# Centred value tiles, regrouped layer-norm steps and rotary partners moved by DMA in a two-block transformer kernel

## The reference

```python
def rotary(x, pos):                 # block 1: all 64 dims of a head, half = 32
    ...
    x1, x2 = x[..., :half], x[..., half:]
    out = jnp.concatenate([x1 * cos - x2 * sin, x2 * cos + x1 * sin], axis=-1)

def retention(q, k, v, g):          # 6 heads of 64
    q, k = rotary(q), rotary(k) * HEAD_DIM ** -0.5
    ...
    y = (y_intra + y_cross).reshape(b, s, RET_HEADS, HEAD_DIM)   # both linear in v
    y = layer_norm(y).reshape(b, s, RET_WIDTH)      # mean and variance over the 64 dims of a head
    return (jax.nn.silu(g) * y)

def hybrid_layer(x, ...):           # block 1
    u = rms_norm(x, g_mix_pre) @ w_in
    aq, ak, av, cu, rq, rk, rv, rg = jnp.split(u, SPLITS, axis=-1)
    mix = jnp.concatenate([chunk_attention(aq, ak, av, rel_bias),
                           conv_module(cu, ...),      # layer_norm over 256, then silu
                           retention(rq, rk, rv, rg)], axis=-1) @ w_out
    x = x + rms_norm(mix, g_mix_post)
    f = jnp.square(jax.nn.relu(rms_norm(x, g_mlp_pre) @ w_up)) @ w_down
    return x + rms_norm(f, g_mlp_post)

def rope(x, pos, rot_dim):          # block 2, NSA: rot_dim = 16 of a head's 64, half = 8
    xr = x[..., :rot_dim]; x1, x2 = xr[..., :half], xr[..., half:]
    rot = jnp.concatenate([x1 * cos - x2 * sin, x2 * cos + x1 * sin], axis=-1)
    return jnp.concatenate([rot, x[..., rot_dim:]], axis=-1)

def second_block(x, ...):           # each of its two layers
    x = x + 0.5 * swiglu(rmsnorm(x, ffn1_norm[l]), ...)
    ...   # mixer: MLA (6 heads), NSA (6 query heads, 2 key heads: compressed, selected, window), stick-breaking (4 heads)
    x = x + 0.5 * swiglu(rmsnorm(x, ffn2_norm[l]), ...)
```

## Time and profile before

| | before |
|---|---|
| median of three runs | 3349.65 us (3349.09 to 3351.13) |
| profiled execution, its own time | 3350.39 us |
| span of the profiled execution | 3348.6 us |
| mixing of block 1, layer 0, to the start of the output product | about 24 to 236 us |
| first layer of block 2: first MLP from, mixing | about 1283 us, 1660 to 1950 us |
| distance from layer 0 to layer 1, block 1 and block 2 | 626 us and 1033 us |

### The profile page before, as it was taken

The page is one execution under the profiler, slowest core; times in us unless marked ns, Lnnn a source line. Parts: engine busy times, 40 slices in busy tenths (PEclk is TensorE's granted clock), DMA queues, the critical chain, the costliest instruction groups (busy, mean ns, idle before and its releaser), DMA issues.

```text
span 3348.6 us, 41894 instructions
## 1 busy us (share of the span) xinstructions
PE 3295.5 (98%) x15570; PEld 2590.8 (77%) x15570; DVE 1673.7 (50%) x2170; ACT 1229.7 (37%) x1842; POOL 245.8 (7%) x268
## 2 busy tenths in 40 slices
PE   9999999999999999999999999999999999999999
PEld 6767888776678887888876788888888876678887
DVE  6755443577544335443656554435443464654434
ACT  4343122433522234223455442334332355543323
POOL 1200000021010000000102300002000101300000
PEclk9999999999999999999999999999999999999999
DMA  7213323321233232332331133333333331033332
GB/s 175 69 48 91 95 95 99 94 82 51 69 103 100 94 106 73 98 97 97 88 75 29 36 103 96 98 94 98 98 94 101 94 82 39 25 90 97 96 96 73
DMA packets 434261, 288.21 MB, mean 86 GB/s; under 512 B 44528, under 2 KB 412316, under 8 KB 433896
## 3 DMA queue, kind: packets, MB, share of 16 engines
q1 hardware_dynamic: 431272, 280.06, 28.8%
q0 software_dynamic: 2736, 4.58, 0.9%
q10 hardware_dynamic: 144, 2.10, 0.2%
HBM read 284.56 MB, written 2.13 MB: 86 GB/s over the span
## 4 chain that ended last, share of the span: by engine, by line
PE 93%; DVE 3%; ACT 2%; issue 1%; DMA 0%; SPq 0%; DVEq 0%; ACTq 0%
PE bank L2077 27%; PE bank L2079 27%; PE bank L2078 27%; PE bank L2240 2%; PE bank L2289 1%; PE bank L2264 1%; PE bank L2370 1%; PE bank L2333 1%; PE bank L2189 1%; ACT wsplit L970 1%; PE bank L2213 0%; PE bank L2101 0%; PE bank L2148 0%; PE bank L2664 0%; PE bank L2396 0%
## 5 line engine op out<-in xcount | busy, mean ns | idle before, releaser
L2077 PE MATMUL bank<-hh,wsplit 128*128 128x512 f32 x2768 | 1093.9, 395 | 10.9 <-DVE wsplit L1451 4.6
L2079 PE MATMUL bank<-hh,wsplit 128*128 128x512 f32 x2768 | 1079.0, 390 | 0.0
L2078 PE MATMUL bank<-hl,wsplit 128*128 128x512 f32 x2768 | 1078.4, 390 | 0.0
L1451 DVE TENSOR_TENSOR wsplit<-raw,wsplit 128x1024 fp32r<-128x1024 f32 (+2 forms) x534 | 645.4, 1210 | 292.9 <-ACT wsplit L970 278.3
L970 ACT ACTIVATE wsplit<-raw 128x1024 fp32r<-128x1024 f32 (+2 forms) x534 | 546.3, 1034 | 262.0 <-PE bank L2079 261.5
L2077 PEld LDWEIGHTS bank<-hh,wsplit 128*128 128x128 f32 x2768 | 520.4, 188 | 136.0 <-issue 22.9
L2078 PEld LDWEIGHTS bank<-hl,wsplit 128*128 128x128 f32 x2768 | 520.6, 188 | 109.9 <-issue 3.1
L2079 PEld LDWEIGHTS bank<-hh,wsplit 128*128 128x128 f32 x2768 | 520.2, 188 | 109.7
L2077 PE MATMUL bank<-fshi,wsplit 128*128 128x512 f32 x1294 | 507.0, 392 | 2.2 <-DVE wsplit L1451 1.4
L2079 PE MATMUL bank<-fshi,wsplit 128*128 128x512 f32 x1294 | 503.6, 389 | 0.0
L2078 PE MATMUL bank<-fslo,wsplit 128*128 128x512 f32 x1294 | 503.5, 389 | 0.0
(11 more groups left out here) (273 smaller groups left out, 2551.5 us busy)
## 6 DMA issues: line engine op xcount, KB each, us to landing
raw<-in_ffn_w_gate SPq DMA_DIRECT2D x88, 512.0 KB, 3.8
raw<-in_ffn_w_up SPq DMA_DIRECT2D x88, 512.0 KB, 3.8
raw<-in_ffn_w_down SPq DMA_DIRECT2D x88, 512.0 KB, 3.5
raw<-in_w_in SPq DMA_DIRECT2D x78, 512.0 KB, 4.0
raw<-in_w_up SPq DMA_DIRECT2D x64, 512.0 KB, 4.0
raw<-in_w_down SPq DMA_DIRECT2D x64, 512.0 KB, 3.3
raw<-in_w_out SPq DMA_DIRECT2D x16, 512.0 KB, 3.7
raw<-in_w_in SPq DMA_DIRECT2D x18, 256.0 KB, 3.3
```

What stands on the lines that cost most here:

```text
L1451: dve.tensor_tensor(slot3(wlo, s, m), slot3(raw, s, m), slot3(whi, s, m).bitcast(F32), ALU.subtract).then_inc(c.lo_done.sem, 1)
L2077: pe.matmul(o, wh, ah, start=start, stop=False)
L2078: pe.matmul(o, wh, al, start=False, stop=False)
L2079: return pe.matmul(o, wl, ah, start=False, stop=stop)
```

## The change

Three things are changed, and both order strings with them.

1. **Joints.** At the start of block 1's MLP and of block 2's first MLP, `hi` of the two units after the first stretch stands ahead of the norm on ACT, and their `lo` ahead of the first evacuations on DVE (`split=4` in block 2; block 2's second MLP stays as it is).
2. **End of block 1's mixing.** The retention's value tile is turned by products with `centre`, the identity minus `blk`, instead of transposes, so that the values and their sums have mean zero in each head. The groups `lm` go. ACT squares bank 7 in `r_out` before it copies it. The steps behind are put in another order: the three norms' groups come earlier, the two units of `ahead` are split, the silu table is loaded once ahead of the convolution's silu, the gate's silu follows, `early` 1 and 2 stand behind it, and the Ln table is loaded once at the end. A piece of attention values moves ahead.
3. **Front of block 2.** For nq0, nq1, nq2 and nks the group `swap` goes. Pool waits for ACT's copy and issues four DMAs of 8 rows each (2 KB a row) from the tile into a scratch tile of two; DVE's `roll` waits for them and does the same three operations. PE waits for `rolled` before the compressed scores (three) and before the first scores (four). nkc and nkw stay as products.

```diff
+ROLLED, ROLL_AT, ROTARY_ROWS = ("q0", "q1", "q2", "ks"), (0, 512), 8
...
-    "bffsfkfkrsekbkfkeyesrftbfcrskktfbfvyrksktefbfvskkkkfercbtyrefvkbkstkffvoseftcvrbhfkkeyhstfvrbhhhehkrhsfktcfhvbehkhstfykv"
...
+    "bffsffkkrkesbkfkeebsrftyfrcsbktfkfvyrkstekfbfvkeskfkkrkctbryvfkteskbffvorbfctvheksekyfhstfrbvherhhhkstchfkfhvbehhsktfhhv"
...
+    c[:, C_CENTRE:C_CENTRE + P] = np.eye(P) - c[:, C_BLK:C_BLK + P]
...
+                add_turned(f"rv{t}", 2432 + 128 * t, t, 4, dst=A_RV, centred=True), ("g", f"sk{t}")]
...
-    prepared += [("mix", 0), gate(0), ("mix", 1), ("g", "lm0"), ("g", "cm"), gate(1), ("mix", 2), ("g", "lv0"), ("c_square",), gate(2), ("g", "cv"), ("g", "lm1"), ("early", 0), ("g", "lv1")]
-    prepared += [("ahead",), ("early", 1), ("g", "lm2"), ("gated",), ("r_square", 2), ("rmul", 0), ("rmul", 1), ("early", 2)]
-    prepared += [("conv_out",), ("mix", 3), ("mix", 4), ("ln_set",), ("g", "lv2"), ("mix", 5), ("mix", 6), ("rmul", 2), ("mix", 7)]
+    prepared += [("mix", 0), gate(0), ("mix", 1), ("g", "cm"), gate(1), ("mix", 2), ("g", "lv0"), ("c_square",), gate(2), ("ahead", 2), ("g", "cv"), ("g", "lv1"),
+                 ("early", 0), ("ahead", 3), ("g", "lv2"), ("silu_set",), ("conv_out",), ("mix", 3), ("mix", 4), ("gated",), ("rmul", 0), ("rmul", 1), ("early", 1), ("early", 2), ("mix", 5), ("mix", 6), ("rmul", 2), ("mix", 7), ("ln_set",)]
...
-    fill += [("g", "snkc"), ("px", 0), nsa_q(0), ("px", 1), compress(0, 0), nsa_q(1), ("g", "snq0"), compress(0, 1), ("px", 2), nsa_q(2),
-             ("g", "snq1"), ("g", "cs0"), compress(1, 0), ("px", 3)]
-    fill += [add("nks", "fm", ("w_in", 1056), frees="act", dst=N_KS), ("g", "snq2"), ("g", "w20"), compress(1, 1)]
-    fill += [add("gatesf", "fm", ("w_gates_pe", 0), frees="act", dst=M_POSX), ("g", "cs1"), ("g", "snks"), ("g", "w21")]
+    fill += [("g", "snkc"), ("px", 0), nsa_q(0), ("px", 1), compress(0, 0), nsa_q(1), ("roll", 0), compress(0, 1), ("px", 2), nsa_q(2),
+             ("roll", 1), ("g", "cs0"), compress(1, 0), ("px", 3)]
+    fill += [add("nks", "fm", ("w_in", 1056), frees="act", dst=N_KS), ("roll", 2), ("g", "w20"), compress(1, 1)]
+    fill += [add("gatesf", "fm", ("w_gates_pe", 0), frees="act", dst=M_POSX), ("g", "cs1"), ("roll", 3), ("g", "w21")]
...
+                pool.wait_ge(c.rn_rstd.sem, c.rn_rstd.at(l, 2))
+                for i, name in enumerate(ROLLED):
+                    made = b2["groups"][f"n{name}"]
+                    pool.wait_ge(c.evac(made).sem, c.emptied(l, made))
+                    if i >= 2:
+                        pool.wait_ge(c.rolled.sem, c.rolled.at(l, i - 1))
+                    for head in (0, HD):
+                        for to, at in ((head, head + ROTARY_ROWS), (head + ROTARY_ROWS, head)):
+                            pool.dma_start(g(ROLL_AT[i % 2], S, (to, to + ROTARY_ROWS)), g(rolled_tile(i), S, (at, at + ROTARY_ROWS))).then_inc(c.roll_in[i % 2].sem, 16)
...
+                        act.activation(g(A_RK + S * s[1]), bank[:, 7, :], ACT.Square).then_inc(c.ret_sq.sem, 1)
                         act.activation(g(A_RQ + S * s[1]), bank[:, 7, :], ACT.Copy).then_inc(c.r_o.sem, 1)
...
-                rms_of_parts(c, l, 3, A1_MLP[1], c.mlp_parts, c.mlp_total, OUT_BANK)
                 for j in range(LOOK, 4):
                     hi(c, b, l, n0 + j + LOOK)
+                rms_of_parts(c, l, 3, A1_MLP[1], c.mlp_parts, c.mlp_total, OUT_BANK)
...
+                for n in range(LOOK, 4):
+                    hi(c, b, l, n + LOOK)
                 if l:
                     rms(c, l, 1, A_FIRST, KT, bank[:, DOWN_BANK, :], D)
                 else:
                     rms_of_parts(c, l, 1, A_FIRST[1], c.in_parts, c.in_total, DOWN_BANK)
-                mlp(l, 0, 0)
+                mlp(l, 0, 0, 4)
...
+            def roll(c, l, i):
+
+                tile, rolled = g(rolled_tile(i)), g(ROLL_AT[i % 2])
+                dve.wait_ge(c.roll_in[i % 2].sem, c.roll_in[i % 2].at(l, 4 * (i // 2) + 4))
+                dve.tensor_tensor(rolled, rolled, tab[:, S:2 * S], ALU.mult).then_inc(c.dve_step.next(), 1)
+                dve.tensor_tensor(tile, tile, tab[:, 0:S], ALU.mult).then_inc(c.dve_step.next(), 1)
+                dve.wait_ge(c.dve_step.sem, c.dve_step.now(l))
+                dve.tensor_tensor(tile, rolled, tile, ALU.add).then_inc(c.rolled.sem, 1)
...
+                    if first:
+                        for j in range(LOOK, 4):
+                            lo(c, b, l, n0 + j + LOOK, i)
                     for j in range(4):
-                        if not (first and j < LOOK):
+                        if not first:
                             lo(c, b, l, n0 + j + LOOK, i)
...
+                pe.wait_ge(c.rolled.sem, c.rolled.at(l, NSA_PAIRS))
...
+                        if gr.get("centred"):
+                            ins = pe.matmul(bk[:, P * t:P * t + P], g(gr["tile"] + P * t, P), centre, start=True, stop=True)
+                        else:
+                            ins = pe.transpose(bk[:, P * t:P * t + P], g(gr["tile"] + P * t, P), ident)
...
-                elif kind == "rmean":
-                    tile = g(A_RQ + S * gr["t"])
-                    dve.tensor_tensor(tile, tile, bk[:, :], ALU.subtract).then_inc(evac, 1)
...
-                elif kind == "rmean":
-                    pe.wait_ge(c.r_o.sem, c.r_o.at(l, 1 + gr["t"]))
-                    ins = pe.matmul(bk[:, :], blk, g(A_RQ + S * gr["t"]), start=True, stop=True)
...
+                    pe.wait_ge(c.ret_sq.sem, c.ret_sq.at(l, gr["t"] + 1))
+                    pe.wait_ge(c.r_o.sem, c.r_o.at(l, gr["t"] + 1))
                     ins = pe.matmul(bk[:, :], blk, g(A_RK + S * gr["t"]), start=True, stop=True)
```

More of the change, by code:

```diff
@@ L57 @@
 C_STACK = C_VALID + 4
-C_WORDS = C_STACK + HD
+C_CENTRE = C_STACK + HD
+C_WORDS = C_CENTRE + P
 SCR_SQ, SCR_RSTD, SCR_TMP, SCR_SQ2 = 0, 1024, 1536, 2560
@@ L657, in counts_of @@
             c.px = signal("px", 0, 4)
+            c.roll_in = [signal(f"roll_in{s}", 0, 2 * len(ROLLED), 0, 16) for s in range(2)]
+            c.rolled = signal("rolled", 0, len(ROLLED))
             c.px_hi = signal("px_hi", 0, 4)
@@ L1313, in _, with mlp @@
             c, b = c2, b2
-            def mlp(l, n0, f0):
+            def mlp(l, n0, f0, split=LOOK):
                 def gated(i, first=False):
@@ L1319, in gated @@
                     for j in range(4):
-                        if not (first and j < LOOK):
+                        if not (first and j < split):
                             hi(c, b, l, n0 + j + LOOK, i)
@@ L1885, in _ @@
                     elif s[0] == "ahead":
-                        for n in range(LOOK, OUT_FIRST + 1):
-                            lo(c, b, l, b["wo"] + n)
+                        lo(c, b, l, b["wo"] + s[1])
                 for m in range(KT):
@@ L1931, in _, with mlp @@
             c, b = c2, b2
-            def mlp(l, n0, f0, d0, r):
+            def mlp(l, n0, f0, d0, r, split=LOOK):
                 def gated(i, first=False, last=False):
                     for j in range(4):
-                        if not (first and j < LOOK):
+                        if not (first and j < split):
                             lo(c, b, l, n0 + j + LOOK, i)
@@ L1971, in _ @@
                 c.dve_step.k = 0
-                mlp(l, 0, 0, 0, 1)
+                for n in range(LOOK, 4):
+                    lo(c, b, l, n + LOOK)
+                mlp(l, 0, 0, 0, 1, 4)
                 dve.wait_ge(c.prm_in.sem, c.prm_in.at(l, 11))
@@ L1992, in _ @@
                         key_pe(c, b, l)
+                    elif s[0] == "roll":
+                        roll(c, l, s[1])
                     elif s[0] == "turn_q":
```

45 lines of the change are left out of this document (21 added, 24 removed).

## The result

| | before | after |
|---|---|---|
| median | 3350.18 us (3349.09 to 3351.13, 4 runs) | 3327.41 us (3326.95 to 3328.22, 4 runs) |
| span of the profiled execution | 3348.6 us | 3325.1 us |

The ratio is 0.9932, with a 95% interval of 0.9915 to 0.995: 22.8 us faster, where 19.1 had been forecast (3330.6, range 3322 to 3343).

A forecast was written before the change was run, and what follows sets the result against it. PE was taken to bound the kernel, busy for 3295.5 of 3348.6 us. The terms 4.1 - 3.3 + 11.8 + 0.7 + 5.8 sum to 19.1 us won, giving 3330.6, range 3322 to 3343.

The forecast's parts named there:

- joints: MLP entries: PE's waits for low parts go, 2.6 us in block 1 and 1.5 in block 2, 4.1 in all.
- turns: Block 1's value tile: three products instead of transposes cost 0.55 us more each, 3.3 in all; maybe nothing at bank waits.
- means and end: Block 1's mixing: removed means and mask wait win 1.7 us a layer, the re-laid end 4.3; 11.8 in all.
- clock: Block 1's mixing end, layer 1: the granted clock of 0.87 costs 1.4 us; half counted as won, 0.7.
- block 2's front: Four permutation products a layer leave PE: 2.9 us a layer won, 5.8 in all, nq1's counted as 0.
- with the variance moved between those scores DVE has time: Block 1's retention scores: the mask waits go, so 1.7 us a layer is won ahead of the end.
- more: Rival: the clock stays at 1.00 also in block 2 and middle waits shrink; 5 us more, 3325.6; chance 0.10.
- signs of being wrong: DVE held over 2 us at roll 0 or 1, PE then waiting for `lo`, output wait over 2.5, or newly lowered clock.
- nothing late behind: Block 2's front: no late engine behind the removed product, so its full 0.96 us is won.
- The open term: Block 2's front: cost of Pool's tile-to-tile transfers, about 2.4 us for four issues and 4.6 to landing, taken as free.
- late-partners rival: Block 2's front: partners land 12.0 us after the last issue, losing 6 a layer; 3342.5; chance 0.10.
- Half the gain lost to other engines: Rival: ACT and DVE chains fill freed PE time in block 1's mixing and block 2's front; 8.8 us lost, 3339.4; chance 0.14.

The follow-up runs named there:

- the kernel with the old letters: The kernel after with block 1's order string as in the kernel before (two f fewer at its end): 3332.1 us, 4.7 slower.
- block 2's old letters: The kernel after with block 2's order string as in the kernel before: 3331.1 us, 3.7 slower.
- the kernel with a wait of 3.03 at the output's first product: The kernel after with the gate's silu and its two products again ahead of the convolution's silu: 3333.4 us, 6.0 slower.
- the products again: The kernel after with the four permutation products back in block 2's front and no transfers by Pool: 3332.6 us, 5.2 slower.
- nq1's product: The kernel after with nq1 alone treated by the permutation product, the other three tiles by transfers: 3328.2 us, 0.8 slower.
- the kernel with the variance earlier: The kernel after with block 1's last variance ahead of the first early product, the fourth output unit's parts behind the mix: 3323.6 us, 3.8 faster.
- the two kernels with all six transfers: The kernel after with nkc and nkw by transfers too: 3328.7 us; the same plus block 1's last variance ahead of the first early product: 3326.9 us.

## Why the prediction was right, and where its terms were off

The middle column is worked out from starts of the same products in the two traces (the first products behind the two post-norms of block 1, the first scores and the latents' norm in block 2), layer by layer; the last one is what an experiment gave for the same part.

| part | forecast | between the two traces | undone alone |
|---|---|---|---|
| joints | 4.1 | 1.6 + 1.6 + 1.8 = 5.0 | 5.0 |
| block 1's mixing: turns -3.3, means and end 11.8 | 8.5 | 3.5 + 3.6 = 7.1 | - |
| clock | 0.7 | 1.3 + 2.3 = 3.7 | - |
| block 2's front | 5.8 | 3.3 + 2.9 = 6.2 | 5.2 |
| block 2's mixing behind the latents' norm | 0 | 0.7 + 0.7 = 1.5 | 1.5, with the old letters |
| orders of letters | 0, within 3 | inside the parts | 4.7 and 3.7 |

The middle column adds up to the 23.5 us of the spans (each figure is rounded by itself). Layer 0 of block 1, for one: its first product behind the post-norm starts at 279.24 in before and at 275.77 in after, 3.5; layer 1's goes from 906.62 to 896.57, 10.0, of which 3.5 are layer 0's, 1.6 the joint between them and 1.3 the clock. Layer 0's 3.5 contain 0.3 that the first input came later in after.

**Joints.** The mechanism held in full: `hi` fitted into ACT's idle time and nothing was late next. The term was too small by a fifth, as a wait costs PE about 0.3 more than its idle time shows.

**Centred turns.** Estimate 0.55, measured 0.51 each from start to start. But they cost 0.8 a layer and not 1.65, since a third is hidden by Pool and of the second one only 0.3 counts. That was inside the "may be nothing" bound, which named a wait for a bank; where it would happen was not foreseen.

**End of block 1.** The chain laid out anew came out nearly to the tenth: output at 12.4 after the last scores (12.8 forecast), ACT's silu at 9.3 (9.8), wait 1.65 (1.6), the gate ready in time. Ahead of it the step failed that said "with the variance moved between those scores DVE has time". The mask's wait did go, but the kernel with the old letters has the same listed steps and waits 4.3 us for the mask: it was the letters. They also brought the wait for Pool (0.42, in two layers). And PE is through with the last scores of layer 0 1.3 later than before (220.21 and 218.94), 0.3 of it from the first input, where the sum had it about as early as before; in layer 1 it loses 1.1 by the same place. This is no wait: from 20 us to these scores PE's waits add up to 1.7 in before and 1.3 in after, the turns take 1.4 more and the mean's product 1.0 less, which nearly cancels. The remaining 1.0 is products that stand further apart; what widens them was not isolated.

**Clock.** "I count half" was a guess between two ends, and layer 1's end came out near the upper one, 1.3 of 1.4: from 860 to 873 the granted clock is now full (first row below).

```profile
860.00:873.00 13.00, 13.00 (x59) 10.74 (x59) 6.62 (x7) 6.59 (x9) 0.00 (x0) 1.00 0.37 105
2765.00:2775.00 10.00, 10.00 (x74) 8.14 (x73) 3.84 (x6) 2.39 (x3) 0.00 (x0) 0.83 0.17 39
```

Not in the sum, but named under "more", was block 2: before, layer 0's clock fell right behind the first scores of the mixing, where PE loses the time in full. From there (1768.26) to the start of the latents' norm (1796.65) it took 28.4 us, in after 26.05 (1751.53 to 1777.58). In after there is one fall, in layer 1, ahead of those scores, the second row above. One of the prediction's own signs of being wrong, a granted clock below 1.00 where it was full, has thus appeared; it costs 0.3 there and is inside the front's 2.9.

**Block 2's front.** Right in the sum, 2.65 a layer instead of 2.9, and at nq1, which turned into a wait of 0.76. At nq2 "nothing late behind" did not hold: PE waits 0.53 for ACT at the next stick-breaking scores, and the 0.96 came out only because a wait of 0.41 ahead of the compressed keys went. Before to after the front gained 0.5 more in each layer, as a wait of 0.34 for ACT's copy of a tile (L1122) is gone; with block 2's old letters it is back, so it is theirs. The open term, the transfers, was taken at 4.6 us to landing from Pool's small loads; tile to tile it is 2.9, and 0.5 for each issue instead of 0.6. The choice of "free" held: DVE has some 4 us to spare and PE more; the late-partners rival needs lateness that no landing here shows. From the first issue of a tile to its last landing DVE was busy for 28 to 98% of the time, with tensor_tensor and scalar_tensor_tensor operations, and the slow landing of which the page "SBUF — State Buffer" of the Trainium skill warns (section "SBUF: two separate sides") did not show: the slowest of 32 landed after 3.9 us.

**The rivals.** Half the gain lost to other engines was wrong for three of the four rolled tiles (at nq2 only in the sum), right for nq1 (as forecast) and for the two that stayed. That the forecast was near is partly chance: the clock was counted 3.0 too low, the joints 0.9, block 2 with its letters 1.9, and block 1's mixing 1.4 too high. Inside block 1's mixing too, turns that cost half of what was counted and an end that won 0.5 more a layer stand against the products that moved apart.

## What to carry to other kernels

Price a wait that goes at its idle time plus what PE needs to get going again, and lay out the chain behind it with the start-to-start distances of the rows; that gave a 12 us stretch to half a us. Moving a small permutation off PE by a transfer pays only where PE has nothing late right behind it: look, product by product, for what the next one waits for, and also two or three products on. Work that is taken away just ahead of a wait only makes the wait longer, and here the clock fell behind the longer one. An order fitted to one set of groups must be fitted again when groups go; undoing the order alone cost nearly as much as undoing a part of the change, a third of it by the clock in block 1's case.

## What the runs showed of the hardware

**Where the clock falls in these traces.** Behind PE's last product, at the end of the span, it falls in every one and costs nothing. At the end of block 1's mixing it fell by waits: in both layers of the kernel with a wait of 3.03 at the output's first product, in one of two with 0.70, 0.73 and 1.70 shortly after one another (before), in one of two with 1.39 ahead of the last scores (block 1's old letters), in none of the 20 layers right behind a single wait of about 1.65 at the output, and in none of the four with 0.18. The other place is around the first scores of block 2's mixing, where most kernels show one fall in one of the two layers, three none and three one in each, and which layer varies without an edit near it. Where it comes ahead of the scores, as in after, with the products again and with nq1's product, it costs 0.3: the products take longer, nearly all of which the wait of 1.52 in front of the scores, missing in just that layer, gives back. From 2640.01 to 2804.42 after takes 164.4 us with such a fall; the kernel with the variance earlier takes 164.1 without one, from 2636.84 to 2800.95.

```profile
1740.00:1752.00 12.00, 12.00 (x83) 9.76 (x82) 5.34 (x7) 2.82 (x4) 0.00 (x0) 0.86 0.15 35
```

```profile
1740.00:1752.00 12.00, 12.00 (x85) 9.78 (x84) 5.70 (x10) 2.71 (x4) 0.00 (x0) 0.86 0.24 51
2770.00:2782.00 12.00, 10.16 (x69) 7.58 (x68) 8.57 (x15) 2.89 (x5) 0.00 (x0) 1.00 0.24 44
...
2779.80 0.49 PE L2268 MATMUL bank<-G,tab 64*128 64x128 f32 x4 [1.52 <-issue]
```

Where it comes behind them, as in before and in the two kernels with all six transfers, PE loses it: 0.5 to 2.9 us. It came there in all four layers whose wait at the first scores is 2.38, and in one of the fifteen where it is 1.52. What decides among the fifteen was not isolated.

**Small transfers from tile to tile.** 8 rows of 2 KB on Pool's queue land 1.8 to 3.9 us after their issue, median 2.9, while the DMA engines are busy for 44 to 71% of the time, mostly with weight loads; the parameter loads from memory (0.5 to 32 KB each) took 4.6.
